# Turning the hidden values of a gated feed-forward by a 16-bit transposing transfer instead of by TensorE

## What is computed

```python
D_MODEL, SEQ, D_FF = 1024, 256, 2816

def swiglu(x, w_gu, w_down):
    g, u = jnp.split(x @ w_gu, 2, axis=-1)
    return (jax.nn.silu(g) * u) @ w_down

def first_block(x, ...):
    f = swiglu(rms_norm(h, ffn1_pre_g[l]), ffn1_w_gu[l], ffn1_w_down[l])
    h = h + 0.5 * rms_norm(f, ffn1_post_g[l])
    m = hybrid_mixer(rms_norm(h, mix_pre_g[l]), ...)
    h = h + rms_norm(m, mix_post_g[l])
    f = swiglu(rms_norm(h, ffn2_pre_g[l]), ffn2_w_gu[l], ffn2_w_down[l])
    return h + 0.5 * rms_norm(f, ffn2_post_g[l])
```

## Time and profile before

| | |
|---|---|
| median of the runs | 1305.1 us |
| span of the profiled execution | 1302.2 us |
| around the span (1305.1 - 1302.2) | 2.9 us |
| TensorE busy | 1296.9 us |
| VectorE busy | 895.2 us |
| ScalarE busy | 707.5 us |
| granted TensorE clock | 1.000 throughout |

### The profile page before, as it was taken

The page is one execution under the profiler, slowest core; times in us unless marked ns, Lnnn a source line. Parts: engine busy times, 40 slices in busy tenths (PEclk is TensorE's granted clock), DMA queues, the critical chain, the costliest instruction groups (busy, mean ns, idle before and its releaser), DMA issues.

```text
span 1302.2 us, 18174 instructions
## 1 busy us (share of the span) xinstructions
PE 1296.9 (100%) x7332; PEld 1102.5 (85%) x7332; DVE 895.2 (69%) x1032; ACT 707.5 (54%) x976; POOL 87.2 (7%) x77
## 2 busy tenths in 40 slices
PE   9999999999999999999999999999999999999999
PEld 7888888987788888888888999888888889998887
DVE  6576556697978755547767567855776766587575
ACT  6464445568746544435766544544467665444451
POOL 0000000000001000000252000000002610000000
PEclk9999999999999999999999999999999999999999
DMA  9685637542376866644655543466666564345562
GB/s 341 212 300 173 203 109 243 159 130 82 129 260 209 276 186 187 190 148 149 204 181 184 172 143 118 146 195 181 191 193 224 166 209 146 111 136 159 178 193 82
DMA packets 64963, 234.42 MB, mean 180 GB/s; under 512 B 7664, under 2 KB 7792, under 8 KB 64752
## 3 DMA queue, kind: packets, MB, share of 16 engines
q1 hardware_dynamic: 62064, 224.42, 53.7%
q10 hardware_dynamic: 2816, 8.84, 1.9%
HBM read 232.19 MB, written 1.05 MB: 179 GB/s over the span
## 4 chain that ended last, share of the span: by engine, by line
PE 94%; DVE 3%; ACT 1%; issue 0%; DMA 0%; POOL 0%; another core or an unknown queue 0%; ACTq 0%; DVEq 0%; POOLq 0%
PE psum L1952 24%; PE psum L1973 23%; PE psum L1953 23%; PE psum L1958 5%; PE psum L2020 5%; PE psum L2005 5%; PE psum L1959 5%; PE psum L2153 2%; PE psum L2407 1%; DVE w_lo L1205 1%; PE psum L2253 1%; PE psum L2393 0%; PE psum L2170 0%; DMA raw<-weights 0%; DVE scores_max L1383 0%
## 5 line engine op out<-in xcount | busy, mean ns | idle before, releaser
L1205 DVE TENSOR_TENSOR w_lo<-raw,w_hi 128x1024 fp32r<-128x1024 f32 x219 | 265.7, 1222 | 127.5 <-ACT w_hi L624 126.0
L624 ACT ACTIVATE w_hi<-raw 128x1024 fp32r<-128x1024 f32 x219 | 230.1, 1055 | 139.7 <-PE psum L1973 105.0
L1952 PE MATMUL psum<-w_hi,x_hi 128*128 128x512 f32 x552 | 217.8, 395 | 0.0
L1953 PE MATMUL psum<-w_hi,x_lo 128*128 128x512 f32 x552 | 214.7, 389 | 0.0
L1205 DVE TENSOR_TENSOR y_lo<-raw,y_hi 128x1024 fp32r<-128x1024 f32 x139 | 168.9, 1221 | 60.7 <-ACT y_hi L624 60.0
L624 ACT ACTIVATE y_hi<-raw 128x1024 fp32r<-128x1024 f32 x139 | 146.4, 1056 | 76.4 <-PE psum L1973 50.5
L1973 PE MATMUL psum<-w_lo,x_hi 128*128 128x512 f32 x552 | 170.1, 389 | 0.0
L1952 PE MATMUL psum<-y_hi,x_hi 128*128 128x512 f32 (+1 forms) x376 | 148.1, 394 | 0.0
L1953 PE MATMUL psum<-y_hi,x_lo 128*128 128x512 f32 (+1 forms) x376 | 146.3, 389 | 0.0
L1952 PEld LDWEIGHTS psum<-w_hi,x_hi 128*128 128x128 f32 x552 | 103.8, 188 | 22.5 <-issue 1.6
L1973 PEld LDWEIGHTS psum<-w_lo,x_hi 128*128 128x128 f32 x552 | 103.6, 188 | 22.0 <-DVE w_lo L1205 0.7
(11 more groups left out here) (219 smaller groups left out, 2286.7 us busy)
## 6 DMA issues: line engine op xcount, KB each, us to landing
raw<-weights SPq DMA_DIRECT2D x406, 512.0 KB, 4.1
probs<-weights SPq DMA_DIRECT2D x8, 512.0 KB, 5.3
probs_t<-weights SPq DMA_DIRECT2D x8, 512.0 KB, 5.0
arena<-gains ACTq DMA_DIRECT2D x7, 512.0 KB, 5.0
arena<-gate_bias ACTq DMA_DIRECT2D x2, 1536.0 KB, 7.4
norm<-x_feat SPq DMA_DIRECT2D x4, 256.0 KB, 5.1
res<-x SPq DMA_DIRECT2D x2, 512.0 KB, 9.0
arena<-lru_w ACTq DMA_DIRECT2D x1, 1024.0 KB, 5.5
```

Source lines behind the costliest of these rows:

```text
L624: act.activation(slot(t)[0], raw_place(t), ACT.Copy).then_inc(hi_ready, 1)
L1205: dve.tensor_tensor(lo, raw_place(t), hi.bitcast(F32), ALU.subtract).then_inc(lo_ready, 1)
L1952: pe.matmul(out_, l_hi, r_hi, start=start, stop=False, skip_group_check=skip)
L1953: pe.matmul(out_, l_lo, r_hi, start=False, stop=False, skip_group_check=skip)
```

## The change

Steps 1 to 8 of each feed-forward, 16 of 22, are turned in another way (`by_transfer`). A float32 is taken as two 16-bit halves. ScalarE copies the 128 x 512 hidden values as 128 x 1024 16-bit numbers into two planes, one with all lower and one with all upper halves (`hidden_pack`). One transposing transfer of eight 128 x 128 blocks of 16-bit numbers (256 KB), on SyncE's queue, turns both planes. ScalarE joins the halves (`hidden_join`), copies the result rounded into `y1_hi` (`joined_copy`), and VectorE subtracts from it (`joined_rest`). Steps 0, 9 and 10 stay with TensorE. VectorE's two products write the hidden values in the order (half of the step, token half) that the planes want, as 128 x 2 x 128.

The pack stands on ScalarE where the copy stood, in step i. The join, the copy and the rest stand in step i + 1, behind `refill(g + 1)`, `refill(g + 2)` and `refill(g + 2)`. The transfer stands on SyncE ahead of the weight tile `gate_tile + 17` (13 or 14 in the first feed-forward up to step 3). TensorE gets a wait for `hidden_ready` at the start of a step, which it had before through the turn.

```diff
@@ -298,7 +299,7 @@
         merged1 = view(18208, TOK, D)
         merge_tmp1 = view(14112, TOK, 512)
         ff_t = view(9984, TOK, FF_STEP)
-        ff_a = view(9984 + 512, TOK, FF_STEP)
+        ff_a = view(9984 + 512, 2, TOK, P)
 
         lp = view(0, N_LP)
         dil_v = view(256, DIL_GROUPS, TOK, 512)
@@ -317,7 +318,10 @@
         merged2 = view(17664, TOK, D)
         merge_tmp2 = view(17664 + 2048, TOK, 512)
 
-        ff_b = view(11008, TOK, FF_STEP)
+        ff_b = view(11008, 2, TOK, P)
+        ff_planes = view(7168, 2 * FF_STEP).bitcast(U16)
+        ff_swapped = view(7680, 2 * FF_STEP).bitcast(U16)
+        ff_joined = view(8192, 2, SEQ)
         pre_rows = [None, view(3328, D), view(2304, D), view(5888, D), view(9472, D)]
 
         def raw_place(t):
@@ -364,6 +368,25 @@
         def norm_count(n, tok, b):
 
             return 4 * n + 2 * tok + b + 1 if n else b + 1
+
+        def by_transfer(i):
+
+            return 1 <= i < FF_STEPS - 2
+
+        def packed_count(f, i):
+
+            return (FF_STEPS - 3) * f + i
+
+        def turned_count(f, i, toks):
+
+            return 4 * f + (1 if i == 0 else i - FF_STEPS + 4) + (toks[0] if len(toks) == 1 else 0)
+
+        def swap_before(f, i):
+
+            ahead = (13 if i == 1 else 14) if f == 0 and i < 4 else 17
+            return At(FFN1_AT, f, FFN2_AT - FFN1_AT) + 6 * i - 2 + ahead
+
+        SWAPS = {swap_before(f, i): packed_count(f, i) for f in range(2) for i in range(1, FF_STEPS - 2)}
 
         def hidden_count(f, i, toks):
@@ -535,6 +561,10 @@
             for t in range(ALL_TILES):
                 if t < KD // 2:
                     sp.dma_start(first_pair(t), x_feat[t, :, :]).then_inc(feat_loaded[t], 16)
+                if t in SWAPS:
+                    sp.wait_ge(hidden_packed, SWAPS[t])
+                    sp.dma_start_transpose(ff_swapped.rearrange("p (b s) -> p b s", s=P), ff_planes
+                                           ).then_inc(hidden_swapped, 16)
                 if PLACE_LAST[t] is not None:
                     sp.wait_ge(lo_ready, PLACE_LAST[t] + 1)
                 sp.dma_start(raw_place(t), weights[t, :, :]).then_inc(raw_loaded[PLACE[t]], 16)
@@ -694,8 +724,30 @@
                 act.activation(ff_t[:, tok, :], psum[:, gate_bank(i, tok), 0:FF_STEP], ACT.Tanh,
                                scale=ff_scale[:, tok:tok + 1]).then_inc(swish_tanh, 1)
 
+            def hidden_pack(f, i):
+
+                act.wait_ge(hidden_ready, TOK * (FF_STEPS * f + i) + TOK)
+                ff = (ff_a, ff_b)[i % 2].rearrange("p a b c -> p (a b c)").bitcast(U16)
+                act.activation(ff_planes.rearrange("p (h n) -> p h n", h=2), ff.rearrange("p (n h) -> p h n", h=2),
+                               ACT.Copy).then_inc(hidden_packed, 1)
+
+            def hidden_join(f, i):
+
+                act.wait_ge(hidden_swapped, 16 * packed_count(f, i))
+                act.wait_ge(hidden_lo, hidden_count(f, i - 1, (0, 1)))
+                act.activation(ff_joined.rearrange("p a b -> p (a b)").bitcast(U16).rearrange("p (n h) -> p h n", h=2),
+                               ff_swapped.rearrange("p (h n) -> p h n", h=2), ACT.Copy).then_inc(hidden_joined, 1)
+
+            def joined_copy(f, i):
+
+                act.wait_ge(hidden_joined, packed_count(f, i))
+                if i > 1:
+                    act.wait_ge(weights_used, At(FFN1_AT, f, FFN2_AT - FFN1_AT) + 6 * i - 2)
+                h = 2 * (i % 2)
+                act.activation(y1_hi[:, h:h + 2, :], ff_joined, ACT.Copy).then_inc(hidden_hi, 1)
+
             def hidden_copy(f, i, toks):
-                act.wait_ge(hidden_turned, hidden_count(f, i, toks))
+                act.wait_ge(hidden_turned, turned_count(f, i, toks))
                 cols = slice(toks[0] * P, (toks[-1] + 1) * P)
                 h = 2 * (i % 2)
                 act.activation(y1_hi[:, h:h + 2, cols], psum[:, 2, :].rearrange("p (a s) -> p a s", s=SEQ)[:, :, cols],
@@ -743,18 +795,25 @@
                     for tok in range(TOK):
                         swish(0, 1, tok, base)
                     refill(base + 7, 1)
+                    hidden_pack(0, 1)
                     refill(base + 8, 1)
-                    hidden_copy(0, 1, (0, 1))
                     refill(base + 9, 1)
                 for i in range(2, FF_STEPS - 1):
                     g = gate_tile(base, i)
                     most = 1 if f == 0 and i < 4 else 2
                     for j in range(4):
                         refill(g + j, most)
+                        if j == 1:
+                            hidden_join(f, i - 1)
+                        if j == 2:
+                            joined_copy(f, i - 1)
                     for tok in range(TOK):
                         swish(f, i, tok, base)
                     refill(g + 4, most)
-                    hidden_copy(f, i, (0, 1))
+                    if by_transfer(i):
+                        hidden_pack(f, i)
+                    else:
+                        hidden_copy(f, i, (0, 1))
                     if i < FF_STEPS - 2:
                         refill(g + 5, most)
                     if f == 0 and i == 2:
@@ -1275,17 +1334,28 @@
 
                 ff = (ff_a, ff_b)[i % 2]
                 n = TOK * (FF_STEPS * f + i)
+
+                def halves(v):
+                    return v.rearrange("p (j s) -> p j s", s=P)
+
                 for tok in toks:
                     dve.wait_ge(swish_tanh, n + tok + 1)
-                    dve.scalar_tensor_tensor(ff[:, tok, :], ff_t[:, tok, :], 1.0, psum[:, gate_bank(i, tok), 0:FF_STEP],
+                    dve.scalar_tensor_tensor(ff[:, :, tok, :], halves(ff_t[:, tok, :]), 1.0,
+                                             halves(psum[:, gate_bank(i, tok), 0:FF_STEP]),
                                              ALU.add, ALU.mult).then_inc(half_swish, 1)
                 for tok in toks:
                     dve.wait_ge(half_swish, n + tok + 1)
                     if i == 0:
                         dve.wait_ge(scale_ready, 2 * (TOK * f + tok) + 2)
-                    dve.scalar_tensor_tensor(ff[:, tok, :], ff[:, tok, :], ff_scale[:, TOK + tok:TOK + tok + 1],
-                                             psum[:, gate_bank(i, tok), FF_STEP:2 * FF_STEP], ALU.mult, ALU.mult
-                                             ).then_inc(hidden_ready, 1)
+                    dve.scalar_tensor_tensor(ff[:, :, tok, :], ff[:, :, tok, :], ff_scale[:, TOK + tok:TOK + tok + 1],
+                                             halves(psum[:, gate_bank(i, tok), FF_STEP:2 * FF_STEP]),
+                                             ALU.mult, ALU.mult).then_inc(hidden_ready, 1)
+
+            def joined_rest(f, i):
+                dve.wait_ge(hidden_hi, hidden_count(f, i, (0, 1)))
+                h = 2 * (i % 2)
+                dve.tensor_tensor(y1_lo[:, h:h + 2, :], ff_joined, y1_hi[:, h:h + 2, :].bitcast(F32), ALU.subtract
+                                  ).then_inc(hidden_lo, 1)
 
             def hidden_rest(f, i, toks):
                 dve.wait_ge(hidden_hi, hidden_count(f, i, toks))
@@ -1328,16 +1397,18 @@
                     swiglu(0, 1, (0, 1))
                     refill(base + 7, 1)
                     refill(base + 8, 1)
-                    hidden_rest(0, 1, (0, 1))
                     refill(base + 9, 1)
                 for i in range(2, FF_STEPS - 1):
                     g = gate_tile(base, i)
                     most = 1 if f == 0 and i < 4 else 2
                     for j in range(4):
                         refill(g + j, most)
+                        if j == 2:
+                            joined_rest(f, i - 1)
                     swiglu(f, i, (0, 1))
                     refill(g + 4, most)
-                    hidden_rest(f, i, (0, 1))
+                    if not by_transfer(i):
+                        hidden_rest(f, i, (0, 1))
                     if i < FF_STEPS - 2:
                         refill(g + 5, most)
                     if f == 0 and i in (5, 6):
@@ -2058,7 +2129,7 @@
                     pe.wait_ge(hidden_ready, TOK * (FF_STEPS * f + i) + tok + 1)
                     for j in range(2):
                         ins = turn(psum[:, 2, j * SEQ + tok * P:j * SEQ + (tok + 1) * P],
-                                   (ff_a, ff_b)[i % 2][:, tok, j * P:(j + 1) * P])
+                                   (ff_a, ff_b)[i % 2][:, j, tok, :])
                 ins.then_inc(hidden_turned, 1)
 
             def ffn(f, first_piece):
@@ -2091,21 +2162,19 @@
                         gate(1, 1, 1, q)
                         if q == 1:
                             turn_hidden(1, 0, both)
-                for tok in both:
-                    down(f, 0, tok, 0)
-                turn_hidden(f, 1, both)
-                for tok in both:
-                    down(f, 0, tok, 1)
+                for j in range(2):
+                    for tok in both:
+                        down(f, 0, tok, j)
```

(17 more changed lines are left out.)

## The result

The changed kernel takes 1296.48 us (median of four runs, 1296.32 to 1296.71) against 1304.63 for the kernel before beside it, so 8.15 us less; the ratio is 0.9939 [0.9925, 0.9953]. Forecast were 1297.3 us and 7.8 less. The spans, 1302.2 and 1294.5 us, differ by 7.7.

What follows compares the result with a forecast made beforehand. TensorE, busy 1296.9 of 1302.2 us, was taken as the bound; 16 turns of 0.49 us removed (7.8) and added work at cost 0 gave 1294.4 of span, plus 2.9, 1297.3 us; 8 in 10: 1295.5 to 1327.

Steps and rivals of the forecast that it cites:

- the turn's room: TensorE, steps 1 to 8 of both feed-forwards: removing the turn wins 0.49 us a step, 7.8 us in all.
- 2.9 us around the span: Whole kernel: the measured median's distance to the profiled span, added to the forecast span of 1294.4 us to give 1297.3.
- 3.0 us of slack: Lateness that TensorE stands in a step before it waits for VectorE's rest: 0.7 us on ScalarE plus 2.3 more.
- The limit of 8.4 us: Largest w that costs nothing; above it TensorE waits at a step's first down tile.
- w: Time from the pack's end to the landing of weight tile 57, held behind the transfer; forecast s + 1.2 = 5.4 us.
- s: Time from the pack's end to the landing of the turned values; 4.2 us taken, bounds 3.4 to 9.0.
- A: Rival: turned values come late at ScalarE's join, TensorE waits at each step's first down tile; slower, chance 0.27.
- A's high row: The late-values rival priced at s = 9.0 us: 29 us more, 1326 us; chance 0.17 up to there.
- Others are alike: Claim that step 7 of the first feed-forward, the one followed in pricing the added work, stands for the other steps.
- B: Rival: lateness just past the limit, TensorE waits about 0.5 us a step, as long as the turn; 1305 us, chance 0.08.
- C: Rival: less than the turn's whole room is won on TensorE, 0.1 to 0.15 us a step less; 1299.5 us, chance 0.08.
- D: Rival: the transfer on SyncE's queue is 131072 pieces of 2 bytes, 1.5 ms a step, many times slower; chance 0.02.

## Why the prediction was right

**The bound and the turn's room.** 0.49 us a step on TensorE, all of it on the path: the steps went from 16.80 to 16.32, also with nothing in the turn's place. 16 x 0.49 = 7.8 was forecast; the span gave 7.7. Two small things next to it were not in the sum: the turn of step 1 in the second feed-forward had waited 0.4 us for VectorE and that went too, and steps 7 and 8 of the first gave 0.33 back. The "2.9 us around the span" was no property of the kernel. Where one execution has both numbers they differ by 1.8 us (1296.32 and 1294.5), so the span of before belonged to a quicker execution than the median; that is why the forecast span, 1294.4, came out to 0.1 us and the forecast time, 1297.3, was 0.8 high. The difference of 7.8 does not hang on it.

**ScalarE and VectorE.** 2.1 us more in a step were forecast, 2.2 measured. The pack is 1.06 us as its row said, the join 1.36 and not 1.06; the sum of the rows would be 2.4, but each overlaps the next by 0.1 us (the split of 492.32 ends at 493.38, the join starts at 493.29). No loss from it, since 0.3 of 3.0 us of slack is small.

**The lateness.** The limit of 8.4 us, or 8.1 with the real join, was right, and it was tested from both sides: w of 5.5 us, of 6.6 to 6.7 (two transfers, usual steps) and of 7.9 (two transfers, step 5 of the first feed-forward, which keeps 0.25 us) cost nothing, 8.2 cost 0.18. Beyond it a step pays what it is late, plus 0.6 us for the late tanh when the step before was late, plus what the clock takes. The value of w was right by luck. I took s = 4.2 and let the tile land 1.2 us behind it. In fact s is 2.7, and the tile is not tied to it: it goes out after the transfer's 1.24 us of issue and then takes its own 4.2 us. Both come to 5.4 or 5.5. At s = 9.0, A's high row, my rule would have named the wrong delay: what decides is the issue on SyncE's queue, which the prediction didn't price apart from the landing. "Others are alike" was not quite so either: step 1 of the second feed-forward, with its late pack and a transfer of 4.9 us, had only 0.4 us left, and with step 7 it is the one that waits as soon as one transfer is added.

**What the transfer takes.** It was 2.7 us against the 4.2 of the sum. The Trainium skill's "DMA: Bandwidth & Descriptors", section "Latency and other measured facts", gives 261 GB/s for a transposing transfer with a non-contiguous middle dimension. By it, as an estimate, 1.0 us would be moving; the trace agrees in so far as 2.7 us leaves room for it, but no run here parts moving from start and end. The Trainium skill's "VectorE: DVE Perf Modes", section "The three transpose paths", gives 1309 ns for one block, and eight of them in a row would be an estimated 10.5 us; eight blocks in one transfer take 2.7 us here. The same page's "Rules for kernel authors" advises TensorE where PSUM will do; here the other way was worth 0.48 us a step, since no engine but TensorE was full.

**The rivals.** A was real, but its point was not reached. One transfer more makes two steps wait, three more make it A, with its place and chain of waits in 12 of 16 steps, and cost 39 us. B, a wait just past the limit, happened in one step in sixteen, with 0.18 us. C is out (steps of 16.32, and 0.43 for a second turn). D is out: 2.7 us, and q1 on the page has 16896 packets more than in the earlier trace rows (78960), which is 1056 for a transfer and not 131072.

## What to carry to other kernels

When one engine has no gap, work taken off it is worth its full room, even if the new way takes ten times as long on others (here some 5 us of ScalarE and transfer for 0.48 on TensorE), as long as its end falls inside the slack between the last copy and the use; work out that slack from the timeline as one number, and follow every queue that the new work stands in. A waiting transfer on a queue that carries other loads is paid by the load behind it: put the one that is wanted soonest ahead of it. Past the limit the loss is more than the first lateness: the late engine is late for its next piece as well, and TensorE's clock can fall behind a wait.

## What the runs showed of the hardware

- A transposing transfer of eight 128 x 128 blocks of 16-bit numbers between two places in SBUF lands 2.7 us after issue (13 of 16) and holds SyncE's queue for 1.24 us; a plain copy of the same 256 KB takes 2.3 and 0.47 us. With a 512 KB load of ScalarE's queue beside it, it took 5.7 us, and 2.9 with that load moved away.
- The hold grows in a full queue: four transfers held SyncE for 5.3 us in most steps and for up to 8.9 in a stretch with a DMA share of 0.93.
- ScalarE copies 1024 16-bit numbers in 1.06 us when it reads every second one and writes them dense (the pack), and in 1.36 us when it reads them dense and writes every second one (the join): only the side of the stride differs, so here it costs when writing and not when reading.
- After TensorE stood for 1.8 us in one step, the next step ran without a gap at a mean granted clock of 0.91 (between 2.4 and 1.2 GHz) and took 18.03 us instead of 16.32. No such step follows the wait of 0.44 us in the changed kernel, and not every long wait has one: with four packs TensorE stood for 2.1 us before 114.69 and the next step kept a clock of 1.00, while it stood for 1.9 us before 545.03 and the next had 0.91.
